# A two-layer decoder kernel: the gathered half of its expert layer taken first, and all gates of the dense half made from one-hots

## The chip, the cores and the metric

The program runs on one core of a Trainium2 chip. The metric is the device time of one execution in microseconds (us), lower is better. TensorE is called PE in the rows, VectorE DVE, ScalarE ACT, GpSimd POOL; SP is the queue that issues most DMAs.

## What is computed

A decoder of two layers over 512 tokens of width 1024, all in fp32. Each layer has three mixers (attention, delta rule, S5), whose results are gated, summed and projected ("combining"), then an expert layer, then a gated embedding. The change is about the combining and the expert layer, cut here to its core:

```python
x = x + (g_a * y_a + g_b * y_b + g_c * y_c) @ w_out          # combining
qry = (xt @ w_query)                                          # 8 heads, two parts of 128
v1, i1 = top_k(qry1 @ keys1, 16); v2, i2 = top_k(qry2 @ keys2, 16)
top_s, pos = top_k(v1[:, None] + v2[None, :], 16)             # 16 of 256 pairs
idx = i1 * 128 + i2                                           # one of 16384 experts
gate = softmax(top_s)
act = gelu(einsum('td,thkd->thk', xt, expert_u[idx]))
out = einsum('thk,thkd->td', gate * act, expert_v[idx])
x = x + out
```

A token thus uses 8 x 16 = 128 rows of `expert_u` and of `expert_v`, of 4 KB each.

## The kernel before

The 512 tokens are four tiles of 128, in two halves. Both halves need the same expert layer, but get it in two ways, at the same time.

- **The dense half** (half 0, tiles 0 and 1) is multiplied with all 16384 experts. These are 128 blocks of 128, two to a pair. `pre(p)` multiplies a pair's blocks of `expert_u` with the tokens (32 matmuls of 256 columns in the profile, L1645); ScalarE takes the gelu into one of 12 buffers (L1838); DVE multiplies by the gates, which are zero where a token has not chosen an expert (`values`, L2029 and L2032); `values(p)` on PE multiplies by the blocks of `expert_v` and sums in four banks (16 matmuls of 512 columns, L1657).
- **The gathered half** (half 1, tiles 2 and 3) fetches the rows that its tokens chose, with indirect DMAs from POOL (L2091): a job is one head of one tile, 16 fetches of 128 rows (512 KB) from each table. `chunk(c)` is four fetches: DVE takes four dot products with u rows (L1990) and, two chunks behind, adds four scaled v rows to x (L1996, L2002); ScalarE's gelu is between (L1805). There are 64 chunks, and rings of 5 buffers for u and for v, so fetching is at most five rows ahead.

`tail_order()` writes one list of steps by hand, and each engine walks the same list and does its part of each step. So the place of a step in the list is its place in each engine's queue, and its DMAs' place in SP's. The steps:

- `gate`, `mix`, `out`: combining. A half is four times three gates (L1549, each a 1 MB panel of weights) and a mix (three products into two banks that DVE reads, L1888, L1892), then four `out` panels (L1577, L1897).
- `norm`, `query`, `score`: normalize, multiply by a 1 MB panel (L1603), multiply by the keys (L1614).
- `choose(k, part)`: one head of one half on DVE, in four parts, from L1918 to L1981: some 50 instructions, one after another.
- `slots`, `hot(q)`: the gates of tile 1 as a matrix [expert, token]. PE transposes the chosen numbers; then for four tokens at a time (a quad) DVE makes two one-hots (L2016, L2018), ScalarE scales one by the gates (L1817), PE multiplies them (L1632), ScalarE copies the product (L1823) and stores 2 MB each 8 quads (L1826). The gates of tile 0 go another way: POOL scatters them one by one into an array in DRAM (L2101), which the mixer phase has filled with zeros (L721).
- `add`: DVE adds the dense sums to x (L2039), in the list behind chunk 56. Behind it come the last chunks and the embedding.

The order now: combining of the dense half; its norm; combining of the gathered half, with all eight heads of the dense half chosen beside it; norm of the gathered half, one head chosen; `slots` and 32 quads, with chunks 0 to 3 and five `pre` among them; seven `pre`; then `values` and `pre` of 64 pairs beside chunks 4 to 55; chunks 56 to 63. A `values(p)` step on DVE gates pair p + 2, if its gelu is there; PE's `values(p)` waits for the gates. The list holds the steps in the ratio of 64 pairs to 52 chunks.

Of the kernel before, what the change touches and what calls it, by code (L numbers as in the profile page):

```python
# [17 lines left out]
F32 = mybir.dt.float32  # L18
# [570 lines left out]
def phase_attend(m, layer):  # L589
# [5 lines left out]
    with ExitStack() as ctx:  # L595
        s = semaphores(m, COMMON + " soft_ready exp_done o_filled o_ready ur_ready scanned x_ready y_done y_read gelu_done zeros_set cells_cleared")
        sb = lambda n, shape, dt=F32: ctx.enter_context(nc.sbuf_tensor(f"{n}_{layer}", shape, dt))
        small = sb("small2", [P, 64])
        zeros = sb("zeros", [P, ZEROS])
# [125 lines left out]
        @block.gpsimd  # L725
        def _(pool):
            nc.gpsimd.memset(zeros[:, :], 0.0).then_inc(s.zeros_set, 1)

# [614 lines left out]
CELLS = P * KEYS * P  # L1343
CELL_OCT = OCT * P
LATE_CHUNKS = 4
# [3 lines left out]
def tail_order():  # L1349
# [7 lines left out]
    order = steps[0] + [("norm", 0), ("query", 0, 0)]  # L1357
    second = iter(steps[1])
    for head in range(PEER_HEADS):
        if head + 1 < PEER_HEADS:  # L1360
            order.append(("query", 0, head + 1))
        order.append(("score", 0, head))
        order += [("choose", head, part) for part in (0, 1)]
        order.append(next(second))
        order += [("choose", head, part) for part in (2, 3)]
        if head >= 2:
            order.append(next(second))
    order += list(second)
    order += [("norm", 1), ("query", 1, 0), ("query", 1, 1), ("score", 1, 0)]
    order += [("choose", PEER_HEADS, part) for part in range(4)]  # L1370
    order += [("score", 1, 1), ("slots",)]
    beside = {}
    for head in range(2, PEER_HEADS):
        at = HEAD_CHUNKS * (head - 1) - (4 if head == PEER_HEADS - 1 else 0)
        beside.setdefault(at - 5, []).append(("query", 1, head))
        beside.setdefault(at - 2, []).append(("score", 1, head))

    def chunk(c):
        out = beside.pop(c, []) + [("chunk", c)]
        head = c // HEAD_CHUNKS + 1  # L1380
        if c % HEAD_CHUNKS < 4 and head < PEER_HEADS - 1:
            out.append(("choose", PEER_HEADS + head, c % HEAD_CHUNKS))
        if c % HEAD_CHUNKS >= 4 and head == PEER_HEADS - 2:
            out.append(("choose", CHOICES - 1, c % HEAD_CHUNKS - 4))
        return out

    pairs = 0
# [846 lines left out]
```

## Time and profile before

| | |
|---|---|
| median of 3 runs | 4261.98 us (4260.22 to 4263.0) |
| the profiled run, its own time | 4251.53 us |
| span of its instructions | 4249.7 us |
| PE busy | 3756.1 us, 88% |
| DVE busy | 2619.1 us, 62% |
| ACT busy | 811.9 us, 19% |
| POOL busy | 1856.3 us, 44% |
| bytes moved by DMA | 1063.93 MB, 250 GB/s on average |

The profile is one execution. Busy time counts instructions that an engine is working on; a matmul's end is modelled, and neighbours overlap, so the time that a row of matmuls costs is read from start to start. Idle time is shown with what ended it. A share of busy time over the whole span mixes stages with different limits, so the stages are read one by one.

### The profile page before, as it was taken

The page shows a single profiled execution, that of the slowest core. Times are in us where ns is not written, and L with a number is a line of the kernel's source. Part 1 is how long each engine was busy: PE and PEld are TensorE (multiplying, and loading weights), DVE is VectorE, ACT ScalarE, POOL GpSimd, SP SyncE. Part 2 cuts the span into 40 slices and gives each one's busy share as a digit, 9 for nine tenths or more (in the row PEclk, how much of TensorE's full clock was granted, in tenths as well). Part 3 has the DMA queues.
Part 4 walks back from the last instruction along what each step waited for, and adds up shares of the span by engine and source line. Part 5 has one row for each costly group of instructions (what it writes and reads, how often), then busy time and mean ns, then how long its engine had stood idle before and what let it go on. Part 6 is the DMA issues. An engine that isn't in the chain of part 4 may idle for free. (4 is left out here: it accounts for less than half of the span.)

```text
span 4249.7 us, 42972 instructions
## 1 busy us (share of the span) xinstructions
PE 3756.1 (88%) x15498; PEld 2778.5 (65%) x15498; DVE 2619.1 (62%) x5356; ACT 811.9 (19%) x1637; POOL 1856.3 (44%) x1714
## 2 busy tenths in 40 slices
PE   8889998978999999993697899989789999999935
PEld 7546787867766666641585467877676666666424
DVE  5765216645577677788657652166456776677876
ACT  2243302224000000000222532022240000000002
POOL 6102004764455455567370020047645554555663
PEclk9889999989999999996798999999899999999967
DMA  3201144558999999999722012345579999999996
GB/s 103 109 30 40 66 139 119 125 142 268 376 406 409 409 407 409 407 397 378 266 82 109 31 39 76 139 119 124 159 253 397 405 410 409 401 409 409 399 381 253
DMA packets 333955, 1063.93 MB, mean 250 GB/s; under 512 B 79152, under 2 KB 96176, under 8 KB 312496
## 3 DMA queue, kind: packets, MB, share of 16 engines
q0 software_dynamic: 184320, 537.08, 34.5%
q1 hardware_dynamic: 132368, 505.22, 31.5%
q10 hardware_dynamic: 17056, 18.88, 1.3%
q8 instruction: 124, 2.03, 0.2%
q14 instruction: 87, 0.71, 0.0%
HBM read 1025.27 MB, written 35.78 MB: 250 GB/s over the span
## 5 line engine op out<-in xcount | busy, mean ns | idle before, releaser
L2091 POOL DMA_INDIRECT u_rows<-in_peer_u,idx_all x512 | 662.7, 1294 | 681.1 <-DVE act_u L1990 564.3
L1657 PE MATMUL bank<-v_tile,shared 128*128 128x512 f32 x2048 | 904.6, 597 | 25.3 <-DVE shared L2032 22.5
L2002 DVE SCALAR_TENSOR_TENSOR x<-v_rows,act_w,x 128x1024 f32<-128x1024 f32 x512 | 657.9, 1285 | 345.0 <-DMA v_rows<-in_peer_v,idx_all 325.9
L2091 POOL DMA_INDIRECT v_rows<-in_peer_v,idx_all x512 | 545.7, 1066 | 402.2 <-DVE x L2002 309.8
L1657 PEld LDWEIGHTS bank<-v_tile,shared 128*128 128x128 f32 x2048 | 392.0, 192 | 476.5 <-issue 444.3
L1990 DVE CUSTOM_DVE_ANT_0 u_rows<-u_rows,h 128x1024 f32<-128x1024 f32 x512 | 609.2, 1223 | 146.1 <-DMA u_rows<-in_peer_u,idx_all 144.7
L2101 POOL DMA_INDIRECT first_cells<-first_gate,cell_all x256 | 412.1, 1610 | 578.0 <-DVEq L1982 465.3
L1645 PE MATMUL bank<-hT,bT 128*128 128x256 f32 x2048 | 454.4, 381 | 0.0
L1645 PEld LDWEIGHTS bank<-hT,bT 128*128 128x128 f32 x2048 | 391.1, 191 | 73.6 <-issue 23.9
L1549 PE MATMUL bank<-hT,ring 128*128 128x256 f32 x1536 | 341.3, 384 | 14.2 <-PEq L150 14.2
L1549 PEld LDWEIGHTS bank<-hT,ring 128*128 128x128 f32 x1536 | 294.3, 193 | 55.9 <-issue 15.8
L1315 POOL TENSOR_TENSOR dn_ct<-dn_lt,mixer_consts 128x512 f32<-128x512 f32 x48 | 64.1, 1336 | 595.7 <-ACT dn_lt L1127 461.2
L1838 ACT ACTIVATE shared<-bank 128x512 f32<-128x512 f32 x128 | 76.1, 595 | 1023.3 <-PE bank L1657 949.8
L1645 PE MATMUL bank<-hT,aT 128*128 128x256 f32 x1024 | 234.7, 383 | 0.0
L1603 PE MATMUL bank<-hT,ring 128*128 128x256 f32 x1024 | 228.8, 383 | 3.5 <-issue 3.5
L1645 PE MATMUL bank<-hT,sT 128*128 128x256 f32 x1024 | 231.5, 379 | 0.0
L1645 PEld LDWEIGHTS bank<-hT,aT 128*128 128x128 f32 x1024 | 196.0, 193 | 38.9 <-issue 14.3
L1603 PEld LDWEIGHTS bank<-hT,ring 128*128 128x128 f32 x1024 | 197.0, 193 | 36.2 <-issue 9.8
L1645 PEld LDWEIGHTS bank<-hT,sT 128*128 128x128 f32 x1024 | 195.0, 190 | 26.0
L1888 DVE TENSOR_TENSOR shared<-shared,bank 128x512 f32<-128x512 f32 x48 | 32.5, 687 | 252.3 <-PE bank L1549 250.9
L1691 PE MATMUL bank<-ring,shared 128*128 128x256 f32 x512 | 129.5, 417 | 39.5 <-issue 37.6
L1670 PE MATMUL bank<-consts,shared 128*128 128x128 f32 x64 | 14.3, 407 | 168.1 <-issue 120.5
(377 smaller groups left out, 4998.9 us busy)
## 6 DMA issues: line engine op xcount, KB each, us to landing
v_tile<-in_peer_v SPq DMA_DIRECT2D x256, 512.0 KB, 7.5
ring<-in_w_in_panels SPq DMA_DIRECT2D x76, 1024.0 KB, 4.9
bT<-in_peer_ut SPq DMA_DIRECT2D x128, 512.0 KB, 7.5
ring<-in_peer_w_query SPq DMA_DIRECT2D x32, 1024.0 KB, 5.0
aT<-in_peer_ut SPq DMA_DIRECT2D x64, 512.0 KB, 6.9
sT<-in_peer_ut SPq DMA_DIRECT2D x64, 512.0 KB, 6.8
ring<-in_ple_w_gate SPq DMA_DIRECT2D x24, 1024.0 KB, 8.4
first_cells<-zeros SPq DMA_DIRECT2D x16, 1024.0 KB, 11.4
```

The source lines that it names most:

```text
L1315: nc.gpsimd.tensor_tensor(heads(ct[:, i % 2, :]), heads(lt[:, i % NT, :]), over(m.c(f"join{JOINS[i // NT]}").unsqueeze(1), (P, DN, P)), AL ...
L1549: ins = mm(bank[:, cols(mt)], a[:, mt * P:(mt + 1) * P], b[:, cols(half)], start=(n == 0), stop=(n == len(groups) - 1))
L1603: ins = mm(bank[:, cols(part)], w[:, k, part * P:(part + 1) * P], m.hT[:, k, cols(half)], start=(k == 0), stop=(k == KD - 1))
L1645: ins = mm(m.banks[2 + p % 2][:, cols(e % 2)], pre_w[e % DENSE][:, k, :], m.hT[:, k, cols(0)], start=(k == 0), stop=(k == KD - 1))
L1657: ins = mm(acc[t][part][:, :], act_pair[p % AHEAD][:, at:at + P], v_tile[:, e % DENSE, part * 512:part * 512 + 512], start=(e == 0), stop= ...
L1691: ins = mm(bank[:, cols(t)], ple_hT[:, k, t * P:(t + 1) * P], w[:, k, :], start=(k == 0), stop=(k == KD - 1))
L1838: f(act_pair[p % AHEAD], m.banks[2 + p % 2][:, :], ACT.Gelu_apprx_tanh).then_inc(s.pre_read, 1)
L1888: tt(sig[:, br, :], sig[:, br, :], bank[:, :], ALU.mult).then_inc(s.vec_read, 1)
L1990: nc.vector.tensor_tensor_reduce(out=u[:, n % RINGS, :], in0=u[:, n % RINGS, :], in1=h[:, t, :], scale=1.0, scalar=0.0, op0=ALU.mult, op1= ...
L2002: stt(out=m.x[:, 2 + t, :], in0=vr[:, n % RINGS, :], scalar=act_w[:, p % 4, i:i + 1], in1=m.x[:, 2 + t, :], op0=ALU.mult, op1=ALU.add).the ...
L2091: nc.gpsimd.indirect_dma_start(out=rows[:, n % RINGS, :], out_offset=None, in_=table, in_offset=bass.IndirectOffsetOnAxis(ap=idx_all[:, t, ...
L2101: nc.gpsimd.indirect_dma_start(out=cells, out_offset=bass.IndirectOffsetOnAxis(ap=cell_all[:, n:n + 1], axis=0), in_=first_gate[:, 0, n:n ...
```

## The change

- The gathered half is combined first, the dense half second. Beside the dense half's combining three heads of the gathered half are chosen, and chunks 0 to 10 run.
- Then come the dense half's norm, chunk 11, and all eight of its heads, each with a `query`, a `score` and (six times) a `pre` between them.
- `slots` and `hot` now cover both dense tiles: 64 quads. A scaled one-hot is made by one `tensor_scalar` for each token on DVE (compare, then multiply by the gate); of each three quads' second one-hots ScalarE makes one, by a square and a relu, and DVE two. Chunks 12 to 15 stand behind quads 15, 31, 47 and 63.
- The scatter, the array of cells, its zeros and the `token` numbers go. The gates come in one 1 MB load for each 8 blocks, the first two of them behind `pre(8)` in SP's list, and one DVE instruction gates a pair.
- Behind the last six `pre` comes chunk 16, and 64 pairs stand beside chunks 17 to 55. The gathered half's fourth head is chosen from chunk 17 on. `add` stays behind chunk 56.
- ScalarE's gelu of a chunk moves behind the next chunk's place in the list. POOL walks the list too.

```diff
             Panels(m, s, []).stream(sp, input_panels(io, layer, "deltanet"))
-            sp.wait_ge(s.zeros_set, 1)
-            n = KEYS // ZERO_PARTS
-            for k in range(ZERO_PARTS):
-                sp.dma_start(io.cells[layer, :, n * k:n * (k + 1), :].rearrange("p e t -> p (e t)").rearrange("p (r z) -> p r z", z=ZEROS),
-                             over(zeros[:, :].unsqueeze(1), (P, n * P // ZEROS, ZEROS))).then_inc(s.cells_cleared, 16)
-            sp.wait_ge(s.cells_cleared, 16 * ZERO_PARTS)
...
-            nc.gpsimd.memset(zeros[:, :], 0.0).then_inc(s.zeros_set, 1)
...
-BLOCKS = P // STORE_T
-ZEROS = 512
-ZERO_PARTS = 8
+BLOCKS = 2 * P // STORE_T
 OCT = 8
 OCT_PAIRS = OCT // 2
-QUADS = P // 4
-HOT_CHUNKS = 4
+QUADS = 2 * P // 4
+HOT_CHUNKS = 17
+ACT_QUAD = 2
+GATES_AFTER = 8
+GATHER, DENSE_HALF = 1, 0
+FIRST_HEADS = 3
+CHOSEN = [(GATHER, head) for head in range(FIRST_HEADS)] + [(DENSE_HALF, head) for head in range(PEER_HEADS)]
+CHOSEN += [(GATHER, head) for head in range(FIRST_HEADS, PEER_HEADS)]
...
-    order = steps[0] + [("norm", 0), ("query", 0, 0)]
-    second = iter(steps[1])
+    place = {what: k for k, what in enumerate(CHOSEN)}
+    choose = lambda half, head: [("choose", place[half, head], part) for part in range(4)]
+    beside = {}
+    for head in range(FIRST_HEADS + 1, PEER_HEADS):
+    def chunk(c):
+        return beside.pop(c, []) + [("chunk", c)]
+
+    g, d = steps[GATHER], steps[DENSE_HALF]
+    order = g + d[0:1] + [("norm", GATHER)] + d[1:2] + [("query", GATHER, 0), ("query", GATHER, 1)] + d[2:3] + [("score", GATHER, 0)]
+    order += choose(GATHER, 0) + d[3:5] + [("score", GATHER, 1)] + choose(GATHER, 1) + d[5:6] + chunk(0) + d[6:7] + chunk(1)
+    begun = 2
+    for n in range(7, 20):
+        order += d[n:n + 1]
+        if n == 10:
+            order.append(("query", GATHER, 2))
+        if n == 11:
+            order += [("score", GATHER, 2)] + choose(GATHER, 2)
+        if n % 4 != 2 and n != 11:
+            order += chunk(begun)
+            begun += 1
+    order += [("norm", DENSE_HALF), ("query", DENSE_HALF, 0), ("query", DENSE_HALF, 1), ("score", DENSE_HALF, 0)] + chunk(begun)
+    begun += 1
+    pairs = 0
     for head in range(PEER_HEADS):
-        if head + 1 < PEER_HEADS:
-            order.append(("query", 0, head + 1))
-        order.append(("score", 0, head))
...
-    beside = {}
-    for head in range(2, PEER_HEADS):
-        at = HEAD_CHUNKS * (head - 1) - (4 if head == PEER_HEADS - 1 else 0)
...
+        order += [("query", DENSE_HALF, head + 2)] if head + 2 < PEER_HEADS else []
+        order += [("score", DENSE_HALF, head + 1)] if head + 1 < PEER_HEADS else []
+        order += choose(DENSE_HALF, head)
+        if pairs < EARLY:
+            order.append(("pre", pairs))
+            pairs += 1
+    order.append(("slots",))
     for q in range(QUADS):
         order.append(("hot", q))
-        if q % (QUADS // HOT_CHUNKS) == QUADS // HOT_CHUNKS - 1:
-            order += chunk(q // (QUADS // HOT_CHUNKS))
-        if q % 5 == 4 and pairs < EARLY:
-            order.append(("pre", pairs))
-            pairs += 1
+        if q % 16 == 15 and begun < HOT_CHUNKS - 1:
+            order += chunk(begun)
+            begun += 1
     order.append(("hot", QUADS))
     for p in range(pairs, AHEAD):
         order.append(("pre", p))
+        if p == GATES_AFTER:
+            order.append(("first_gates",))
+    while begun < HOT_CHUNKS:
+        order += chunk(begun)
+        begun += 1
+    for n, what in enumerate([("query", GATHER, FIRST_HEADS), ("score", GATHER, FIRST_HEADS)] + choose(GATHER, FIRST_HEADS)):
+        beside.setdefault(begun + n, []).append(what)
...
+                pe.wait_ge(*right_made(q))
                 if q >= 2:
                     pe.wait_ge(s.hot_read, q - 1)
                 for i in range(4):
...
+            def gate_oct(k):
+                if k >= 2:
+                    sp.wait_ge(s.gated, OCT_PAIRS * (k - 1))
+                sp.dma_start(gates[:, k % 2, :], dram[:, k].rearrange("p b e t -> p (b e t)")).then_inc(gate_in[k % 2], 16)
+
+            def first_gates():
+                for k in range(2):
+                    sp.wait_ge(stored[k], 16 * BLOCKS // 2)
+                for k in range(2):
+                    gate_oct(k)
...
+                c -= 1
+                if 0 <= c < CHUNKS:
                     act.wait_ge(s.u_free, STEP * (c + 1))
                     f(act_g[:, c % 4, :], act_u[:, c % 4, :], ACT.Gelu_apprx_tanh).then_inc(s.gelu_done, 1)
...
+                k = q + 2
+                if k < QUADS and by_act(k):
+                    if k >= 4:
+                        act.wait_ge(s.hot_filled, k - 3)
+                    tile, at = k // (P // 4), 4 * k % P
                     for i in range(4):
-                        at = 4 * q + i
-                        f(left[q % 4][:, i, :], left[q % 4][:, i, :], ACT.Copy, scale=turned_sel[:, 2, at:at + 1]).then_inc(s.left_scaled, 1)
+                        f(right[k % 4][:, i, :], m.c("iota"), ACT.Square, scale=-1.0, bias=turned_sel[:, tile, 0, at + i:at + i + 1]).then_inc(s.right_squared, 1)
+                    act.wait_ge(s.right_squared, 4 * right_made(k)[1])
+                    f(right[k % 4], right[k % 4], ACT.Relu, scale=-1.0, bias=1.0).then_inc(s.right_acted, 1)
...
-                at = 4 * q
-                tt(left[q % 4], over(turned_sel[:, 1, at:at + 4].unsqueeze(2), (P, 4, P)),
-                   over(m.c("iota").unsqueeze(1), (P, 4, P)), ALU.is_equal).then_inc(s.left_ready, 1)
-                tt(right[q % 4], over(turned_sel[:, 0, at:at + 4].unsqueeze(2), (P, 4, P)),
-                   over(m.c("iota").unsqueeze(1), (P, 4, P)), ALU.is_equal).then_inc(s.right_ready, 1)
+                tile, at = q // (P // 4), 4 * q % P
+                for i in range(4):
+                    ts(left[q % 4][:, i, :], m.c("iota"), turned_sel[:, tile, 1, at + i:at + i + 1], first_gate[:, tile, at + i:at + i + 1],
+                       ALU.is_equal, ALU.mult).then_inc(s.left_ready, 1)
+                if not by_act(q):
+                    tt(right[q % 4], over(turned_sel[:, tile, 0, at:at + 4].unsqueeze(2), (P, 4, P)),
+                       over(m.c("iota").unsqueeze(1), (P, 4, P)), ALU.is_equal).then_inc(s.right_ready, 1)
...
-                    a = act_pair[p % AHEAD].rearrange("p (e t) -> p e t", e=2)
-                    g = gates[:, o % 2, 0:CELL_OCT].rearrange("p (e t) -> p e t", e=OCT)[:, at:at + 2]
-                    tt(a[:, :, 0:P], a[:, :, 0:P], g, ALU.mult).then_inc(s.gated, 1)
+                        v.wait_ge(gate_in[o % 2], 16 * (o // 2 + 1))
+                    a = act_pair[p % AHEAD].rearrange("p (e b t) -> p e b t", e=2, t=STORE_T)
+                    g = gates[:, o % 2, :].rearrange("p (b e t) -> p e b t", b=BLOCKS, e=OCT)[:, at:at + 2]
                     tt(a, a, g, ALU.mult).then_inc(s.gated, 1)
...
-            def scatter(n):
-                nc.gpsimd.indirect_dma_start(
-                    out=cells, out_offset=bass.IndirectOffsetOnAxis(ap=cell_all[:, n:n + 1], axis=0),
-                    in_=first_gate[:, 0, n:n + 1], in_offset=None, compute_op=ALU.add,
-                ).then_inc(m.scattered, 16)
...
+            def norm(half):
+                if half == GATHER:
+                    for n in range(RINGS):
+                        fetch(n, s.u_free, u, tables[0], m.u_landed)
+                    for n in range(RINGS):
+                        fetch(n, s.v_free, vr, tables[1], m.v_landed)
+
+            def chunk(c):
                 for n in range(STEP * c + RINGS, STEP * (c + 1) + RINGS):
                     fetch(n, s.u_free, u, tables[0], m.u_landed)
                 for n in range(max(STEP * (c - LAG), 0) + RINGS, STEP * (c - LAG + 1) + RINGS):
                     fetch(n, s.v_free, vr, tables[1], m.v_landed)
```

## Rows read from the trace of the kernel before

**Rows 1.** Table of stretches: us, length, busy time by engine, PEclk, DMA share, GB/s.

```profile
2762.00:3004.00 242.00, 219.70 (x1009) 191.94 (x1008) 144.54 (x562) 51.70 (x90) 153.58 (x96) 0.95 0.50 126
...
3030.00:3046.00 16.00, 0.21 (x2) 0.00 (x0) 15.19 (x64) 2.41 (x7) 4.87 (x4) 0.63 0.10 0
...
3046.00:3147.00 101.00, 81.66 (x445) 72.31 (x446) 77.84 (x158) 60.91 (x174) 58.88 (x44) 0.91 0.83 278
...
3203.00:3940.00 737.00, 737.00 (x2633) 497.46 (x2632) 528.92 (x991) 56.34 (x134) 386.05 (x335) 1.00 1.03 407
...
4050.00:4098.00 48.00, 0.30 (x1) 0.00 (x0) 36.88 (x47) 0.82 (x4) 30.82 (x27) 0.55 1.01 396
```

**Rows 2.** Timeline, TensorE, dense sums: start us, us, engine, line, operation.

```profile
1405.19 7.03 PE L1657 MATMUL bank<-v_tile,shared 128*128 128x512 f32 x16
...
1412.05 7.07 PE L1645 MATMUL bank<-hT,bT 128*128 128x256 f32 x32
...
1418.96 7.03 PE L1657 MATMUL bank<-v_tile,shared 128*128 128x512 f32 x16
```

**Rows 3.** Timeline, TensorE and DVE, from the last pre to add, second layer.

```profile
3945.01 34.50 PE L1657 MATMUL bank<-v_tile,shared 128*128 128x512 f32 x80
...
4043.17 7.13 PE L1657 MATMUL bank<-v_tile,shared 128*128 128x512 f32 x16 [1.41 <-DVE shared L2032]
...
3944.76 0.15 DVE L1996 TENSOR_TENSOR act_w<-act_g,gate_all 128x4 f32<-128x4 f32 x1
...
4097.46 2.48 DVE L2039 TENSOR_TENSOR x<-x,bank 128x512 f32<-128x512 f32 x4
```

**Rows 4.** Timeline, TensorE and DVE: end of the first combining, first two choices.

```profile
2732.55 29.58 PE L1577 MATMUL bank<-ring,shared 128*128 128x256 f32 x128 [2.90 <-DVE shared L1892]
...
2787.51 0.87 DVE L1918 MAX8 sel_v<-scores 128x8 f32<-128x128 f32 x4 [15.82 <-ACT scores L1793]
...
2803.52 0.87 DVE L1918 MAX8 sel_v<-scores 128x8 f32<-128x128 f32 x4
```

**Rows 5.** Timeline, DVE: first and last instructions of a mix beside choosing.

```profile
2835.66 1.28 DVE L1888 TENSOR_TENSOR shared<-shared,bank 128x512 f32<-128x512 f32 x2 [0.22 <-DVE first_gate L1981]
...
2842.13 0.69 DVE L1892 TENSOR_TENSOR shared<-shared 128x512 f32<-128x512 f32 x1
```

**Rows 6.** Timeline, DVE: the first instruction of chunk 56.

```profile
4087.23 1.22 DVE L1990 CUSTOM_DVE_ANT_0 u_rows<-u_rows,h 128x1024 f32<-128x1024 f32 x1
```

**Rows 7.** Timeline, DVE, then TensorE: norm, choice, first one-hot, last query, first values.

```profile
3009.47 1.29 DVE L1905 SCALAR_TENSOR_TENSOR h<-x,small,gain_ffn 128x1024 f32<-128x1024 f32 x1
...
3029.59 0.87 DVE L1918 MAX8 sel_v<-scores 128x8 f32<-128x128 f32 x4 [15.77 <-ACT scores L1793]
...
3045.31 0.69 DVE L2016 TENSOR_TENSOR gain_ffn<-turned_sel,consts 128x512 f32<-128x512 f32 x1
...
3147.42 7.07 PE L1603 MATMUL bank<-hT,ring 128*128 128x256 f32 x32
...
3202.68 7.03 PE L1657 MATMUL bank<-v_tile,shared 128*128 128x512 f32 x16
```

**Rows 8.** Timeline, ScalarE, then TensorE: quads of one-hots.

```profile
3053.39 1.27 ACT L1817 ACTIVATE gain_ffn<-gain_ffn,turned_sel 128x128 f32<-128x128 f32 x4
...
3055.03 1.27 ACT L1817 ACTIVATE gain_ffn<-gain_ffn,turned_sel 128x128 f32<-128x128 f32 x4
...
3068.68 2.08 PE L1632 MATMUL bank<-shared,gain_ffn 128*128 128x128 f32 x8 [2.01 <-ACT gain_ffn L1817]
...
3071.05 2.08 PE L1632 MATMUL bank<-shared,gain_ffn 128*128 128x128 f32 x8 [0.30 <-ACT gain_ffn L1817]
```

**Rows 9.** DMA issues: source, queue, count, KB each, median us to landing.

```profile
dense_gates<-v_tile ACTq DMA_DIRECT2D x4, 2048.0 KB, 11.2
```

**Rows 10.** A DVE cast in the timeline, and a group of POOL (busy, mean ns).

```profile
3035.53 0.20 DVE L1935 CAST sel_if<-sel_i 128x64 f32<-128x64 uint32 x1
...
L2091 POOL DMA_INDIRECT u_rows<-in_peer_u,idx_all x512 | 662.7, 1294 | 681.1 <-DVE act_u L1990 564.3 <-issue 96.9 <-DVEq L1982 19.9
```

More of the change, by code:

```diff
@@ L1368, in tail_order @@
[L1368 to L1371, printed above, removed]
-    beside = {}
-    for head in range(2, PEER_HEADS):
-        at = HEAD_CHUNKS * (head - 1) - (4 if head == PEER_HEADS - 1 else 0)
[L1375 to L1385, printed above, removed]
@@ L1387, in tail_order @@
-    pairs = 0
+    place = {what: k for k, what in enumerate(CHOSEN)}
+    choose = lambda half, head: [("choose", place[half, head], part) for part in range(4)]
+    beside = {}
+    for head in range(FIRST_HEADS + 1, PEER_HEADS):
+        at = HEAD_CHUNKS * (head - 1) - (4 if head == PEER_HEADS - 1 else 0)
+        beside.setdefault(at - 5, []).append(("query", GATHER, head))
+        beside.setdefault(at - 2, []).append(("score", GATHER, head))
+        for part in range(4):
+            beside.setdefault(at + part, []).append(("choose", place[GATHER, head], part))
@@ L1482, in phase_tail @@
         ple_hT = comb
+        normed = [ple_h, h]
+        rank = lambda half: 1 - half
+        done = lambda half, head: (s.selected if half == GATHER else s.first_chosen, head + 1)
         act_pair = [shared[:, k, :] for k in range(AHEAD)]
@@ L1526, in slot, with by_act, right_made @@
             return t, head * TOPK + n % TOPK
+        def by_act(q):
+            return q % 3 == ACT_QUAD
+        def right_made(q):
+            mine = len([k for k in range(q + 1) if by_act(k) == by_act(q)])
+            return (s.right_acted if by_act(q) else s.right_ready), mine
         def arrivals(n):
@@ L1558, in mix @@
             def mix(half, pair):
-                if half == 0 and pair == 0:
+                if rank(half) == 0 and pair == 0:
                     pe.wait_ge(s.wg_in, 16)
@@ L1571, in out @@
                 if n == 0:
[L1572 removed]
+                    pe.wait_ge(s.comb_ready, KD // 2 * (rank(half) + 1))
                 w = panel()
@@ L1582, in norm @@
             def norm(half):
-                for t in range(2 * half, 2 * half + 2):
-                    pe.wait_ge(s.h_ready, t + 1)
+                for t in range(2):
+                    pe.wait_ge(s.h_ready, 2 * rank(half) + t + 1)
                     for part, banks in ((0, to_act), (1, to_vec)):
@@ L1593, in query @@
             def query(half, head):
-                if half == 0 and head == 0:
+                if rank(half) == 0 and head == 0:
                     pe.wait_ge(s.keys_in, 16 * 2)
@@ L1613, in score @@
                         at = 2 * t + part
-                        ins = mm(bank[:, at * KEYS:(at + 1) * KEYS], qry[:, head % 2, part * HALF_T + t * P:part * HALF_T + (t + 1) * P], keys[:, part, :],
+                        ins = mm(bank[:, at * KEYS:(at + 1) * KEYS], qry[:, CHOSEN.index((half, head)) % 2, part * HALF_T + t * P:part * HALF_T + (t + 1) * P], keys[:, part, :],
                                  start=True, stop=True)
@@ L1751, in _ @@
             loads = iter(range(len(sources)))
-            parts = {"gate": panel, "mix": panel, "out": panel, "query": panel, "embedded": panel, "pre": pre, "values": values, "add": add}
+            parts = {"gate": panel, "mix": panel, "out": panel, "query": panel, "embedded": panel, "pre": pre,
+                     "first_gates": first_gates, "values": values, "add": add}
             for what, *n in order:
@@ L1764, in gate @@
             def gate(half, pair, br):
-                if br == 0 and half + pair:
-                    act.wait_ge(s.comb_ready, KD // 2 * half + pair)
+                if br == 0 and rank(half) + pair:
+                    act.wait_ge(s.comb_ready, KD // 2 * rank(half) + pair)
                 bank = banks.take()
@@ L2117, in _ @@
                     fetch(n, s.v_free, vr, tables[1], m.v_landed)
-                if c < LATE_CHUNKS:
-                    for n in range(TOPK // LATE_CHUNKS):
-                        scatter(late + c * TOPK // LATE_CHUNKS + n)
+            parts = {"norm": norm, "chunk": chunk}
+            for what, *n in order:
+                if what in parts:
+                    parts[what](*n)
     clear(nc, s)
```

131 lines of the change are left out of this document (38 added, 93 removed).

## The prediction

> **What bounds the kernel now.** All times are those of the second layer in the profiled run, unless another is said; both layers run alike. The first view is the table of stretches [rows 1]. From 3203 to 3940 (the dense sums) TensorE is busy 737 of 737 us and DMA moves 407 GB/s: both are full. Which of them binds is read in TensorE's timeline [rows 2]: a pair's values take 6.86 us (1405.19 to 1412.05) and a pair's `pre` 6.91 us, and they follow each other without a gap. The sum agrees: 51 values, 51 `pre`, five queries of 6.91 and five scores of about 0.9 are 742 us, and the last `pre` ends at 3945.0 [rows 3], 742.3 us behind the first values at 3202.7 [rows 7]. So up to the last `pre` TensorE sets the pace and DMA only just keeps up. Behind it this turns: 13 values (89 us) are left, but DVE is in the middle of chunk 46 (its `act_w`, the eleventh from the end of chunk 56 backwards) and must end chunk 56 before `add`. TensorE ends at 4050.3 and `add` starts at 4097.5, 152.5 us behind the last `pre` [rows 3]: 14.4 us for each of 10.5 chunks, DMA at 396 GB/s to the end [rows 1]. These 63 us beyond TensorE's work are all that chunks cost in this stage. In front of the dense sums the chain is: combining (TensorE), norm and first queries, choosing (DVE), one-hots, seven `pre`.
>
> **The change, part by part.** I place each step on the second layer's clock.
>
> *Combining.* The gathered half is combined first; its cost is unchanged, to 2762.1 [rows 4]. Then one gate panel (32 matmuls as a `pre`, 6.9 us) goes in front of the norm, one behind it and one behind the two queries; of these 21 us about 5 cover the norm's wait. The first choice thus starts not at 2787.5 but near 2803.5. From there DVE is the longer engine: three choices at 16.0 us (2787.51 to 2803.52 [rows 4]) are 48.1; four mixes, each 7.2 us when TensorE's third product must wait for DVE to read a bank (2835.66 to 2842.8 [rows 5]), 28.8; four sums of `out`, 2.8; chunks 0 and 1 have only a u part, 4.6 each, 9.2; chunks 2 to 10 at 10.2 us (4087.23 to 4097.46 [rows 3, 6]), 91.8; the norm 2.8; one wait of 7 for the second head's score. That is 190.5, to 2994. TensorE's own work is 219.7 us in the old stretch less five queries and scores (5 x 7.9), 180 us, so to 2942: DVE binds. DMA has 11 chunks (47 MB with what is ahead in the rings) and some 18 panels (19 MB) in 183 us, 88% of what 409 GB/s would carry; I add 8 us for waits: 3002. Transposes, two queries and the score then take as long as before (DVE's norm to the choice, 3010.8 to 3029.6, 18.8 us [rows 7]), with chunk 11 under them: the dense half's first choice starts at 3021, where one starts now at 3029.6. Minus 9, with ends of minus 34 (25 less, somewhat under half the gap to TensorE's pace) and minus 3 (6 us more of DMA waits).
>
> *Choosing.* Now one choice stands between 3029.6 and the one-hots at 3045.3 [rows 7]; the seven other dense heads are hidden beside the second combining. After the change all eight stand there and nothing else fills DVE: 8 x 16.02 = 128.2, plus 112.5 us. TensorE does six queries and six `pre` under them, about 15.0 us a head, so DVE stays the longer. The extra sums of `chosen` and `listed` swap one for one. Slots: now hidden behind the last choice; then six transposes and two copies, 2.5 us by the 0.6 us copies, plus 2.5.
>
> *One-hots.* Now 32 quads, four chunks and five `pre` take 102.1 us, 3045.3 to 3147.4 [rows 7]. Alone a quad costs 1.64 us, 3053.39 to 3055.03, ScalarE's four scalings and one copy [rows 8]. After: 64 quads. ScalarE has a copy (0.5) each and in one of three four squares (1.27, the row of the scalings) and one relu over 512 (0.6, the copy's row) with a wait: 1.25 a quad. DVE has four 128x128 `tensor_scalar` each and in two of three a 128x512 comparison (0.6 between starts). The trace has no such `tensor_scalar`; below it stands the 128x64 cast at 0.20 [rows 10], of which about 0.1 is apart from the next; above it half the comparison's step, 0.3. I take 0.2, near the casts, for 1.2 a quad. Storing bounds it too: eight stores of 2 MB, 11.2 us to landing [rows 9], over two buffers, so a block of eight quads needs 11.7 us. Three chunks of 10.2 stand between quads (the fourth behind the last); four buffers hide 3 us of each. Five blocks at 11.7, three at 17: 110, and 2 us of lower clock after each chunk: 116. Bounds: 100 if nothing but 1.25 a quad and 20 us of chunks count, 167 below. Plus 14.
>
> *To the first values.* Seven `pre`, 48.4 us, as now; the query that stands there (3147.42 [rows 7]) is gone, minus 6.9. The gates load earlier in SP's order, but SP waits there for the last store (11.2 us) and has 2 MB to bring, all under four `pre`; where SP stands, only weights of `pre` 9 are queued behind, needed 20 us later. Cost nothing; 10 us if that cover is short. The removed scatter of tile 0's gates (POOL's 128 issues a layer) and the clearing of its array in DRAM lie beside other work: nothing. First values: 3202.7 - 9 + 112.5 + 2.5 + 14 - 6.9 = 3315.7, plus 113.
>
> *The dense sums.* 39 chunks instead of 52, but the same values, `pre` and five queries: 742 us to the last `pre`. DMA would need 306 MB, 750 us for the whole, so it has slack there and the slack is worth nothing. One gating instruction instead of two frees only DVE. The gain is behind the last `pre`: there DVE stands at chunk 48 or 49. It can't be further ahead, since ScalarE's gelu of a chunk now sits behind the next chunk, and ScalarE follows TensorE's `pre`. Eight chunks at 14.4 are 115, less 12 to 15 us for rings that are full: `add` starts 100 us after the last `pre` instead of 152.5. Minus 52; bounds minus 62 (TensorE's 90 us) and minus 34 (no ring ahead).
>
> *After `add`* nothing changes (152 us).
>
> *Sum.* Per layer 113 - 52 = +61, twice +122: 4251.5 + 122 = 4373.5 for a run like the profiled one, whose own time lies 10.5 us under the median of three; so 4384.
>
> **The rivals.**
> *TensorE paces the new combining* (faster). For it: it is the busy engine there now (219.7 of 242). It would take the dense half's first choice to 2963, 58 us before my 3021, and one-hots at their lower bound, 16 us less: 61 - 74 = -13 a layer, 4384 - 148 = 4236. It turns the sign only from 61 us on; DVE's 190 us of listed work against 180 speak against it. 14%.
>
> *One-hots at TensorE's lower level, 1.2 of 2.4 GHz* (slower still). The granted clock is 0.63 in the stretch of the choice and 0.91 beside the one-hots, where five `pre` of 6.9 us lie between quads [rows 1]. After short idle times there a quad's eight matmuls take 2.08 us and the quads come 2.37 us apart [rows 8], against 1.64 else. The change takes every `pre` out of this stage. 64 x 2.37 = 152 and 15 for chunks are 167: +51 a layer, 4486. 12%. The Trainium skill (TensorE: Matmul & The Clock Gate, What's actually happening) says the lower level is the default and activity releases it; the rows agree.
>
> *No saving behind the last `pre`.* If DVE's lead is lost or rings are empty: +18 (the bound) to +52 a layer, 4420 to 4488. 7%.
>
> *`tensor_scalar` and POOL's issues hold each other up.* Some 34 gather issues of about 1.2 us [rows 10] fall among 256 of the new instructions; if each issue stops DVE, up to 41 us of DVE time a layer, of which I count 30 on the path: 4444. 7%. The Trainium skill (SBUF — State Buffer, SBUF: two separate sides) says that Vector instructions in a two-port mode and GpSimd lock each other out of a shared port; the trace of before has no such pair to check it.
>
> *It comes out even*: TensorE's pace in the combining alone, the one-hots as forecast, 4384 - 116 = 4268. 6%.
>
> **Numbers.** Forecast 54%, 4384. A measurement here can tell 0.2% from no change. Faster 14%, same 6%, slower 80%. My own case with its bounds: combining -25, one-hots -16, tail -10 a layer gives 4282; +6, +20 and +18 gives 4472. The range leaves out the first rival and the even case: 4295 to 4490.
>
> **What would show it.** Eight choices of 16 us in a row on DVE with TensorE at 90% and DMA almost still; first values 100 to 130 us later in each layer; the same 742 us from there to the last `pre`, with DMA under 400 GB/s; `add` within 15 us of TensorE's last values. I am wrong if the dense half's first choice starts much before 3000, if the one-hots take under 100 us or over 150, or if the stage with `pre` gets shorter than 742, for then DMA was binding it.

## The result and the profile after

The changed kernel takes 4495.75 us (median of 4, 4488.75 to 4500.43) against 4261.1 for the one before: ratio 1.055, 95% interval 1.0532 to 1.0568. The forecast was 4384 (4295 to 4490): the direction held, the size was half of what came, and the time lies above the range. The profiled run took 4500.43 us (span 4498.5) where the one of before took 4251.53 (span 4249.7): 248.8 us more in the span, 126.2 by the end of the second layer's first combining and 122.6 behind it. As the layers run alike, all that follows is the second layer, read from that point on (2762.1 before, 2888.1 after).

The table of stretches of the changed kernel shows the stages in order (us; length; busy time of TensorE, its weight loads, DVE, ScalarE, POOL; granted clock; DMA share; GB/s), to be held against [rows 1]:

```profile
2888.00:3117.00 229.00, 184.07 (x809) 158.96 (x808) 148.98 (x336) 47.75 (x72) 92.55 (x76) 0.90 0.71 265
3117.00:3163.00 46.00, 21.40 (x93) 18.39 (x92) 31.24 (x41) 6.96 (x13) 25.21 (x23) 0.70 0.98 369
3163.00:3288.00 125.00, 90.40 (x445) 79.97 (x444) 117.04 (x488) 32.07 (x64) 0.00 (x0) 0.87 0.28 103
3288.00:3413.00 125.00, 73.37 (x513) 68.69 (x513) 122.80 (x341) 74.39 (x175) 31.57 (x25) 0.83 0.62 219
3413.00:3482.00 69.00, 51.11 (x227) 44.32 (x226) 36.33 (x51) 4.87 (x9) 34.59 (x27) 0.85 0.91 347
...
3482.00:4223.00 741.00, 741.00 (x2647) 499.61 (x2646) 410.81 (x766) 55.11 (x122) 316.11 (x247) 1.00 0.89 343
4223.00:4346.00 123.00, 90.11 (x211) 39.63 (x209) 80.69 (x107) 2.11 (x10) 73.37 (x61) 0.88 1.03 409
```

While eight heads are chosen and while the one-hots are made, DVE is busy 240 of 250 us and DMA moves 103 and 219 GB/s. In the sums TensorE is full and DMA has 16% to spare (343 GB/s, of the 409 that it moves in the stage behind), where it was full before (407). Bytes were moved out of the stage that could carry them into stages where DVE pays for them.

By the prediction's steps, in us of the second layer:

| step | before | predicted | after |
|---|---|---|---|
| end of first combining to the dense half's first choice | 267.5 | 258.5 | 275.0 |
| choices and slots, to the first one-hot | 15.7 | 130.7 | 125.7 |
| one-hots | 102.1 | 116 | 124.1 |
| to the first values | 55.3 | 48.4 | 68.9 |
| dense sums to the last `pre` | 742.5 | 742 | 741.6 |
| last `pre` to `add` | 152.3 | 100 | 122.8 |
| `add` to the end | 152.2 | 152 | 152.1 |

Four rows are off by 16.5, 8, 20.5 and 23 us to the worse, and one by 5 to the better. The four are taken in turn.

*Front.* DVE's timeline at the end of the combining (start us, us, engine, line, operation, in brackets the idle time before it and what ended it):

```profile
3117.91 1.28 DVE L2008 SCALAR_TENSOR_TENSOR x<-v_rows,act_w,x 128x1024 f32<-128x1024 f32 x1
3120.37 1.28 DVE L2008 SCALAR_TENSOR_TENSOR x<-v_rows,act_w,x 128x1024 f32<-128x1024 f32 x1 [1.18 <-DMA v_rows<-in_peer_v,idx_all]
...
3140.01 1.28 DVE L1919 SCALAR_TENSOR_TENSOR shared<-x,small,gain_ffn 128x1024 f32<-128x1024 f32 x1
...
3163.32 0.87 DVE L1932 MAX8 sel_v<-scores 128x8 f32<-128x128 f32 x4 [7.42 <-ACT scores L1807]
```

and what DVE waited for from its first choice to the norm, 207 us (us in all, times, longest):

```profile
DVE sel_v L1932 <- ACT scores L1807: 36.1, 2, 28.6
DVE shared L1902 <- PE bank L1558: 13.1, 4, 3.3
DVE x L2008 <- DMA v_rows<-in_peer_v,idx_all: 8.6, 7, 2.4
DVE u_rows L1996 <- DMA u_rows<-in_peer_u,idx_all: 7.9, 8, 1.6
```

Gathered rows held DVE up for 16.5 us, not the 8 that were added for it. (The 28.6 in the first line is the wait in front of the first choice.) TensorE was done with its last `out` product at 3117.6 and idled 23.8 us.

*One-hots.* DVE's timeline among the quads (x4: four instructions in a row):

```profile
3294.91 1.11 DVE L2023 TENSOR_SCALAR gain_ffn<-consts,turned_sel,first_gate 128x128 f32<-128x128 f32 x4
3295.94 0.69 DVE L2026 TENSOR_TENSOR shared<-turned_sel,consts 128x512 f32<-128x512 f32 x1
3296.54 1.11 DVE L2023 TENSOR_SCALAR gain_ffn<-consts,turned_sel,first_gate 128x128 f32<-128x128 f32 x4
3297.57 1.11 DVE L2023 TENSOR_SCALAR shared<-consts,turned_sel,first_gate 128x128 f32<-128x128 f32 x4
3298.59 0.68 DVE L2026 TENSOR_TENSOR shared<-turned_sel,consts 128x512 f32<-128x512 f32 x1
```

Four `tensor_scalar` are 1.03 us from start to start (3294.91 to 3295.94), 0.257 each where 0.2 was taken, and with two comparisons of 0.6 in three quads a quad is 1.43 on DVE. 64 x 1.43 are 91.3; three chunks of 10.2 come on top in full, since DVE itself is the longest engine: 122. The stores, by which the prediction paced the stage (11.2 us to landing), took 7.7 in the median (the profile's page has it for one of the two buffers), and no engine waited for one in this stage.

*To the first values.* The chain of waits, in order of time:

```profile
3413.91 23.13 DMA dense_gates<-gates
...
3437.05 0.02 SPq L1745
...
3437.12 0.33 SPq L1741
...
3437.49 0.43 SPq L1741
...
3437.96 13.76 DMA bT<-in_peer_ut
...
3451.86 30.31 PE bank L1657 x128
```

The last store needed 23.1 us beside the gathers of two chunks. SP stood in `first_gates` until then, and the weights of `pre` 9 were issued behind 2 MB of gates and took another 13.8. TensorE idled 17.9 us and its next `pre` took 9.59 us instead of 7.07, at a granted clock of 0.50 (the lower level) while it had idled.

*Behind the last `pre`.* It ends at 4223.6 with DVE in chunk 49 (a `u` row, its four `v` rows and chunks 50 to 56 are left, 7.7 chunks), as forecast. But these took 122.8 us, 16.0 each, not 14.4.

### The profile page after: what moved, and what is told of

Its sections match the earlier page's. It is cut to its first block and busy times, and to the rows that moved or that the text cites. A ratio compares the mean times of both kernels' runs of the same rounds, so it can differ in the third digit from the quotient of the medians.

```text
span 4498.5 us, 44058 instructions
## 1 busy us (share of the span) xinstructions
PE 3840.9 (85%) x16016; PEld 2854.8 (63%) x16016; DVE 2700.5 (60%) x5614; ACT 877.4 (20%) x1677; POOL 1523.2 (34%) x1456
## 5 line engine op out<-in xcount | busy, mean ns | idle before, releaser
L2096 POOL DMA_INDIRECT u_rows<-in_peer_u,idx_all x512 | 679.8, 1328 | 1610.4 <-DVE act_u L1996 988.5
L2096 POOL DMA_INDIRECT v_rows<-in_peer_v,idx_all x512 | 608.0, 1188 | 626.3 <-DVE x L2008 488.6
L1996 DVE CUSTOM_DVE_ANT_0 u_rows<-u_rows,h 128x1024 f32<-128x1024 f32 x512 | 603.3, 1223 | 91.3 <-DMA u_rows<-in_peer_u,idx_all 81.9
L2002 DVE TENSOR_TENSOR act_w<-act_g,gate_all 128x4 f32<-128x4 f32 x128 | 20.3, 159 | 471.7 <-ACT act_g L1820 471.7
L361 PE MATMUL bank<-ring,hT 128*128 128x256 f32 x640 | 151.4, 398 | 0.0
```

What stands on the lines that cost most here:

```text
L361: ins = nc.tensor.matmul(bank[:, 0:PANEL], m.hT[:, k, r::4], w[:, k, :], start=(k == 0), stop=(k == KD - 1))
L1996: nc.vector.tensor_tensor_reduce(out=u[:, n % RINGS, :], in0=u[:, n % RINGS, :], in1=h[:, t, :], scale=1.0, scalar=0.0, op0=ALU.mult, op1= ...
L2096: nc.gpsimd.indirect_dma_start(out=rows[:, n % RINGS, :], out_offset=None, in_=table, in_offset=bass.IndirectOffsetOnAxis(ap=idx_all[:, t, ...
```

## Experiments

A ratio is the time over that of the kernel before, measured beside it. Differences from the changed kernel are taken from two ratios; each has an interval of some 8 us to either side, so a difference of 16 us is one only roughly. What a stage takes is read from the second layer of each trace.

### Gates later in SP's list

```
-GATES_AFTER = 8
+GATES_AFTER = 11
```

> The changed kernel, but the first two loads of gates stand behind pre(11) in SP's list and not behind pre(8). Theory, the place in the list: SP stands there for the last store (issued at 3413.9, landed at 3437.0), and pre 9's weights are queued behind it and behind 2 MB of gates, so that TensorE idles 17.9 us and runs the next pre slower. With the loads three pre later the store has landed before SP comes to them: first pre of the run to first values 50 to 52 us instead of 68.9, 18 us less a layer, 4460. Rival, the bytes: 2 MB of gates, the chunks' gathers and the weights must all come in before the first values, and DMA is the limit wherever they stand: the stall moves to the first values, 4490 to 4500.

Measured: 4470.56 us, ratio 1.0509 (1.0491 to 1.0527), against 1.055 for the changed kernel: 17 us less, and 28 less between the profiled spans. First `pre` to first values 54.9 us instead of 68.9. SP's and TensorE's rows:

```profile
3429.24 0.80 SPq L1741 DMA_DIRECT2D gates<-dense_gates  x2
```

```profile
3444.06 6.32 PE L1657 MATMUL bank<-hT,aT 128*128 128x256 f32 x16 [3.64 <-DMA aT<-in_peer_ut]
```

The gates are issued without standing behind the store, and the stall of 17.9 is 3.6. So the place in the list was the larger part of the 20.5 us. The rest is probably bytes (389 GB/s in this stretch); no run separates it. The expected 18 us a layer was 14.

### Fewer chunks behind the last pre

```
-        goal = min(PAIRS_ALL, -(-(c - HOT_CHUNKS + 1) * PAIRS_ALL // (DENSE_END - HOT_CHUNKS)))
+        goal = min(PAIRS_ALL, PAIRS_ALL if c >= DENSE_END else -(-(c - HOT_CHUNKS + 1) * SPREAD // (DENSE_END - HOT_CHUNKS)))
```

with `SPREAD = 54`.

> The changed kernel, but chunks 17 to 55 are spread over 54 pairs instead of 64, so that 4 chunks instead of 9 stand behind the last pre in the list. Theory: the stage before the last pre has DMA to spare (343 of 409 GB/s), and behind it a chunk costs only its own bytes, 4.2 MB or 10.3 us, over a fixed 44 us of values and panels. 742 us to the last pre as before at some 385 GB/s, then TensorE's 13 values bind: add 93 us behind the last pre instead of 122.9, 30 us less a layer, 4436. Rival: DMA has no real slack there, since gathers and loads hold each other up: the stage to the last pre grows by what the end loses, 4485 to 4500.

Measured: 4428.69 us, ratio 1.0412 (1.0394 to 1.0429), 59 us less than the changed kernel by the ratios. The stretches up to the last `pre` and from there to `add`:

```profile
3445.00:4186.00 741.00, 741.00 (x2648) 499.60 (x2647) 468.07 (x839) 55.67 (x128) 371.59 (x293) 1.00 0.97 378
4186.00:4276.00 90.00, 89.74 (x211) 39.59 (x209) 25.48 (x37) 0.88 (x4) 22.01 (x18) 1.00 0.80 302
```

The sums take the chunks at no cost, with 378 GB/s, and `add` follows TensorE's last values at once. So DMA's slack in front of the last `pre` is real. What is behind it goes by bytes: one fixed part and 10.3 us (4.2 MB at 409 GB/s) for each chunk. Before, 152.3 us went to 10.5 chunks, after, 122.8 to 7.7: 10.5 us a chunk, with 42 to 44 us left at none (13 MB of values alone are 33 us at 409 GB/s). Two points always give a line, but the other orders lie on it too. 44 us and 10.3 a chunk make 131.6 for the 8.5 chunks left in the next two experiments, which took 133.2 and 132.3; and 117.1 and 120.2 for the 7.1 and 7.4 left in the runs of the kernel before with its chunks earlier and with five chunks among its quads, which took 116.4 and 119.9. Only the run with three chunks beside the `pre`s lies off, 116.4 for 7.6 chunks where the line has 122.3. With the few chunks left in this run TensorE's 90 us bind.

### Quads without chunks

```
-HOT_CHUNKS = 17
+HOT_CHUNKS = 13
```

> The changed kernel, but chunks 12 to 14 don't stand between the 64 quads of one-hots and chunk 16 not behind the last pre's: they go with the dense sums (43 chunks there instead of 39). Theory: DVE is the longest engine of the one-hots (1.43 us a quad), so each chunk there costs its full 10.3 us: stage of 94 us instead of 124. The sums have DMA to spare, so the moved chunks cost nothing before the last pre and one more of them, 10 us, behind it: 20 us less a layer, 4456. Rival, bytes are conserved: what leaves the one-hots comes back behind the last pre, 4490 to 4500. Rival, TensorE: without work between them the quads fall to 2.37 us each, stage 150, 4550.

Measured: 4444.36 us, ratio 1.0446 (1.0428 to 1.0463), 44 us less than the changed kernel. The one-hots:

```profile
3263.00:3357.00 94.00, 68.35 (x507) 64.03 (x508) 93.95 (x304) 71.15 (x168) 0.92 (x1) 0.94 0.47 157
```

DVE is busy in all of the 94 us: it is the pace, and each of the three chunks had cost its 10 us. TensorE kept a clock of 0.94, so the rival of the lower level is out. The last `pre` to `add` grew by 10.4 us, the price of the one chunk more. The run beats the 4456 expected: without the chunk behind the last `pre`s, first `pre` to first values took 61.4 us instead of 68.9.

### Four chunks less beside the combining

```
-        if n % 4 != 2 and n != 11:
+        if n in (7, 8, 9, 12, 13):
```

with `HOT_CHUNKS = 13`.

> The changed kernel, but with 7 chunks beside the dense half's combining instead of 11; the one-hots keep their three, so 43 chunks stand with the dense sums. Theory: DVE paces the combining (TensorE's last out product ends at 3117.5, DVE comes to the norm at 3140.0, with 16 us of waits for gathered rows between). With four chunks less DVE is done before TensorE: the norm comes some 19 us earlier and then TensorE binds; one more chunk behind the last pre costs 10: 9 us less a layer, 4478. Rival, the waits for the score and the banks pace it: front unchanged, 10 us more a layer, 4516.

Measured: 4469.3 us, ratio 1.0513 (1.0496 to 1.0531), 16 us less than the changed kernel. TensorE's last `out` product ends 229.2 us behind the first combining in both; but the norm follows it at once:

```profile
3102.81 0.69 DVE L1911 TENSOR_TENSOR x<-x,bank 128x512 f32<-128x512 f32 x1 [6.22 <-PE bank L1586]
3106.32 0.16 DVE L1918 RECIPROCAL small<-small 128x1 f32<-128x1 f32 x1 [2.82 <-ACT small L1792]
```

The dense half's first choice comes at 254.3 instead of 275.0. So at 11 chunks DVE binds, at 7 TensorE does. But its pace isn't that of the prediction's rival, which had the choice at 201 (2963 on the clock of before): TensorE, whose work is some 180 us, needs 229 to its last `out` product, above all since in each mix it waits for DVE to read a bank. The last mix, in the changed kernel and in this one:

```profile
3081.52 3.58 PE L1558 MATMUL bank<-sT,ring 128*128 128x256 f32 x8 [10.22 <-DVE shared L1902]
```

```profile
3066.50 3.78 PE L1558 MATMUL bank<-sT,ring 128*128 128x256 f32 x8 [10.69 <-DVE shared L1902]
```

Four such waits are 36 us (10.2, 8.4, 7.2 and 10.2 in the changed kernel), with or without chunks between. The combining in the new order (229, with three queries in it) is shorter than in the old (242, with eight); it is the chunks laid on it that make the front longer.

### The new gates in the old order

The changed kernel with `tail_order` of the kernel before, 64 quads with a `pre` behind every tenth, chunks behind quads 15, 31, 47 and 63, and

```
-        normed = [ple_h, h]
-        rank = lambda half: 1 - half
+        normed = [h, h]
+        rank = lambda half: half
```

> The changed kernel's gates (64 quads with tensor_scalar, no scatter, one gating instruction, late gelu) in the order of the kernel before: the dense half first, seven of its heads chosen beside the second combining, four chunks beside the quads, five or six pre's among them. It splits the change. Theory: DVE paces the quads, 64 x 1.43 and 30 for three chunks and 16 for a head's choice, 138 us, then six pre's with the stall at the gates, 60: 198 us from the first one-hot to the first values instead of 157, 41 us a layer, and nothing else moves: 4254 + 82 = 4336. So 82 of the change's 234 us would be the gates and the rest the order. Rival, the old scatter and the second gating instruction cost something on the path: 4300 or less.

Measured: 4346.61 us, ratio 1.0204 (1.0187 to 1.0221); expected 4336. From the first one-hot to the first values 203.7 us against 157.3, of which 154.1 are up to the first `pre` behind the quads. The rest is smaller: last `pre` to `add` 156.3 against 152.3, the second combining 236.6 against 242.2. The stretches from the first one-hot to that `pre`, and from the last `pre` to `add`:

```profile
3090.00:3244.00 154.00, 118.40 (x736) 108.57 (x737) 135.07 (x401) 77.65 (x177) 42.55 (x34) 0.92 0.74 251
...
4036.00:4193.00 157.00, 94.53 (x210) 40.45 (x208) 123.89 (x182) 6.01 (x18) 102.31 (x84) 0.83 1.02 402
```

So the gates (with the late gelu) cost 88 of the change's 234 us, and the new order the other 146.

### The kernel before: chunks earlier in the sums

> The kernel before, with its 52 chunks spread over 58 pairs instead of 64, so that 8 chunks instead of 12 stand behind the last pre: the edit that gained 30 us a layer in the changed kernel. Theory, here DMA is full on both sides of the last pre (407 and 396 GB/s): what the end gains the stage before it loses, last pre some 20 to 30 us later, add in its place: 4254. Rival, only DVE's lead sets the 152 us at the end: add 111 us behind the last pre and that one in its place, 4172.

The edit is that of the changed kernel's `goal` in the second experiment, with `SPREAD = 58` beside the old constants. Measured: 4265.48 us, ratio 1.0014 (1.0005 to 1.0024). Up to the last `pre`, and from there to `add`:

```profile
3212.00:3996.00 784.00, 752.27 (x2656) 506.80 (x2655) 575.30 (x1069) 62.03 (x144) 431.14 (x365) 0.98 1.02 402
3996.00:4113.00 117.00, 95.17 (x210) 40.66 (x208) 78.42 (x114) 2.04 (x8) 74.80 (x59) 0.93 1.03 409
```

784.7 instead of 742.5, then 116.4 instead of 152.3, 6 us more together: what gains 30 us a layer in the changed kernel gains nothing here and costs a little, since DMA has nothing to spare. The Trainium skill (Perfetto Trace Analysis, Roofline) puts the ceiling of one core's DMA engines at about 435 GB/s. The traces here stay below it: stretches of 100 us, laid every 20 us over all the runs, reach 411 at most, with DMA's share at 1.03. For these transfers, rows gathered beside loads, 409 is the figure to plan with.

### The kernel before: chunks into its own gaps

```
+    begun = HOT_CHUNKS
     for p in range(pairs, AHEAD):
         order.append(("pre", p))
+        if p in BESIDE_PRE:
+            order += chunk(begun)
+            begun += 1
```

with `BESIDE_PRE = (6, 8)` and the sums' `goal` spread over 61 pairs.

> The kernel before, with chunks 4 and 5 beside the last pre's in front of the dense sums (behind pre(6) and pre(8)), and the sums' list spread so that 10 chunks stand behind the last pre instead of 12. In that stretch (3147 to 3203) DVE waits 44 us and DMA moves 270 of 409 GB/s. Theory, the sums with their end are a matter of bytes there (364 MB at 407 GB/s): two chunks less are 8.4 MB, 20 us a layer: 742 us to the last pre as before, add 132 behind it instead of 152, 4214. Rival, the chunks' gathers delay the gates and weights of the first values by as much: 4254, no change.

Measured: 4226.56 us, ratio 0.993 (0.9913 to 0.9946). The stretch in front of the first values and the two behind:

```profile
3129.00:3196.00 67.00, 64.39 (x308) 56.60 (x307) 37.63 (x60) 9.35 (x23) 37.51 (x29) 1.00 0.97 365
3196.00:3939.00 743.00, 742.71 (x2657) 501.18 (x2658) 542.99 (x1029) 59.50 (x140) 397.15 (x337) 1.00 1.03 408
3939.00:4071.00 132.00, 98.72 (x208) 41.61 (x206) 93.03 (x131) 2.33 (x10) 81.74 (x70) 0.90 1.01 400
```

19.8 us less behind the last `pre`, as expected; 6 of them are given back between the first one-hot and the first values (163.6 against 157.3), so 4214 was missed by 13 us.

> The kernel before, with three chunks beside the last pre's (behind pre(6), pre(8) and pre(10)) instead of the two of the earlier run, 9 chunks behind the last pre. With two, DMA moved 366 GB/s in that stretch: 60 us x 43 GB/s are 2.6 MB, less than a chunk's 4.2. Theory, bytes: the third brings 0 to 6 us a layer over the two (4226 there against 4258 for the kernel before): 4214 to 4226. Rival, the third holds up the weights of the last pre's: first values 10 us later, 4240 or more.

With `BESIDE_PRE = (6, 8, 10)` and `SPREAD = 60`: 4213.78 us, ratio 0.9901 (0.9885 to 0.9918), at the better end of what was expected. Against two chunks there the sums get 6 us longer and their end 16 shorter.

> The kernel before, with five chunks between its 32 quads instead of four (behind quads 6, 12, 18, 24 and 31) and two beside the last pre's. Beside those quads DVE is busy 78 of 101 us and ScalarE paces them (1.64 us a quad), and DMA moves 278 GB/s, so a chunk isn't paid in full there, unlike in the changed kernel: theory 5 us for the fifth chunk against 10 us of bytes less behind, 4216. Rival, a chunk there costs its 10.3 us as in the changed kernel: 4226, as with two beside the pre's alone.

```
-HOT_CHUNKS = 4
+HOT_CHUNKS = 5
+HOT_AT = (6, 12, 18, 24, 31)
...
-        if q % (QUADS // HOT_CHUNKS) == QUADS // HOT_CHUNKS - 1:
-            order += chunk(q // (QUADS // HOT_CHUNKS))
+        if q in HOT_AT:
+            order += chunk(HOT_AT.index(q))
```

With `BESIDE_PRE = (7, 9)` and `SPREAD = 60`: 4200.89 us, ratio 0.9872 (0.9856 to 0.9888), the fastest of all. One-hots, `pre`s, sums, and their end:

```profile
3019.00:3119.00 100.00, 80.21 (x431) 70.84 (x432) 85.34 (x175) 58.40 (x166) 70.06 (x51) 0.90 0.89 305
3119.00:3183.00 64.00, 58.63 (x285) 51.69 (x284) 32.34 (x48) 9.09 (x23) 29.48 (x25) 0.99 0.98 382
3183.00:3927.00 744.00, 744.00 (x2648) 500.73 (x2648) 545.29 (x1034) 58.93 (x139) 403.45 (x339) 1.00 1.02 406
3927.00:4047.00 120.00, 95.82 (x210) 40.89 (x208) 80.78 (x113) 2.13 (x9) 71.79 (x61) 0.91 1.03 410
```

The fifth chunk lengthens the one-hots by 3 to 6 us and not by 10.3: up to the `pre` in front of the last quad they take 99.8 us, against 93.4 in the kernel before and 96.6 in the run with two chunks beside the `pre`s, both with four chunks. DVE has 15 of 100 us to spare even now, where it has 2 of 125 in the changed kernel. From the first one-hot to the first values it is 163.2 us, as in that run (163.6), so all told the chunk came free, and 4216 was beaten by 15 us. The end of the sums is 32 us shorter than before.

### All four edits on the changed kernel

```
-HOT_CHUNKS = 17
+HOT_CHUNKS = 9
-GATES_AFTER = 8
+GATES_AFTER = 11
+SPREAD = 58
...
-        if n % 4 != 2 and n != 11:
+        if n in (7, 8, 9, 12, 13):
```

and the `goal` of the second experiment.

> All four edits on the changed kernel at once, five chunks deeper: gates behind pre(11), seven chunks beside the combining, none among the quads, one beside the last pre's, 47 with the dense sums, spread so that the last seven stand behind the last pre. Theory, the savings add up until DMA is full: front 254 (from the end of the gathered half's combining to the choice), 126 choosing, 95 quads, 52 to the first values, 742 and 91 for 339 MB at 407 GB/s, 152 at the end: 1512 us a layer where the kernel before has 1488: 4303. Rival, at that fill gathers and loads hold each other up: the sums with their end take 860, 4360.

Measured: 4325.6 us, ratio 1.0164 (1.0147 to 1.0181).

```profile
3324.00:4066.00 742.00, 742.00 (x2652) 500.29 (x2651) 513.82 (x900) 56.10 (x133) 391.18 (x330) 1.00 1.01 401
4066.00:4169.00 103.00, 91.26 (x208) 39.46 (x206) 64.18 (x86) 1.60 (x7) 58.13 (x49) 0.95 1.03 409
```

The savings add up (some 165 of the 234 us come back) until DMA is full; sums and end take 845 us where 833 were forecast. What stays is the bare choosing, 110 us a layer; the front (254.9 against 267.5), the one-hots with the `pre`s behind them (143.4 against 157.3) and the sums with their end (845 against 895) give back 76 of it.

## Why the prediction was right in sign and wrong in size

The sum per layer was forecast at 61 us and came to 122.6. The bounds by stage were right (DVE in the combining and the choosing, TensorE in the sums) except in the one-hots. The terms that failed are, by size, the end of the sums (23 us short), the loads of gates in front of the first values (20.5), the waits in the combining (16.5) and the one-hots (8).

*What bounds the kernel before.* Right, and its consequence was drawn too weakly. "DMA only just keeps up" was shown to be a limit: chunks earlier in the sums gain nothing. The 63 us "beyond TensorE's work" are bytes.

*Combining: minus 9, measured plus 7.5.* That DVE binds was right. The rival in which TensorE paces was priced far too high (58 us less than the forecast): with four chunks less it does pace, and comes to 254.3, 4 us less than the forecast, as it waits 36 us for banks. In the forecast itself the term that failed is the waits: the first choice came 3.5 us later than worked out, gathered rows held DVE 16.5 us instead of 8, and the two queries behind the norm took 15.9 us instead of 14, TensorE having idled 23.8 us (granted clock 0.70 in that stretch). That is 14 of the 16.5 us; the rest is spread over small waits.

*Choosing: plus 115, measured plus 110.* Right; eight heads without a mix between them are 15.4 us each, not 16.0. Slots plus 2.6, as forecast.

*One-hots: plus 14, measured plus 22.* The `tensor_scalar` was taken as 0.2 from a 128x64 cast and is 0.257. The larger fault is which resource binds: the stage was paced by stores at 11.2 us each, though two buffers give a store the time of the next block to land, and half of each chunk was hidden under them. The stores held nobody up, DVE binds, and chunks there are paid in full. That the total is off by 8 us only is luck: DVE needs 11.4 us for a block of eight quads (8 x 1.43), nearly the 11.7 that the stores had been given, so the chunks, 15 us too cheap, are what is left, less the 6 us put down to a lower clock. The rival of the lower clock did not come: TensorE had 0.83 here and its quads are not the longest.

*The port rival* is out. Four `tensor_scalar` beside POOL's issues of gathers, in DVE's timeline and in POOL's:

```profile
3322.19 1.11 DVE L2023 TENSOR_SCALAR gain_ffn<-consts,turned_sel,first_gate 128x128 f32<-128x128 f32 x4
3323.22 0.69 DVE L2026 TENSOR_TENSOR shared<-turned_sel,consts 128x512 f32<-128x512 f32 x1
```

```profile
3322.00 1.09 POOL L2096 DMA_INDIRECT v_rows<-in_peer_v,idx_all  x1 [0.30 <-issue]
3323.39 1.32 POOL L2096 DMA_INDIRECT v_rows<-in_peer_v,idx_all  x1 [0.31 <-issue]
```

The four take 1.03 us to the next instruction beside POOL as without it. Over the stage all of DVE's rows of four last 1.11 or 1.12 us, but one (1.20), and there are 25 of POOL's issues in it. Whether they run in the mode of which the Trainium skill (SBUF — State Buffer, SBUF: two separate sides) says that it locks POOL out, no run here shows.

*First values: minus 6.9, measured plus 13.6.* The prediction named the queue and what stands in it ("only weights of `pre` 9 are queued behind, needed 20 us later") and the price if the cover is short, 10 us. The step that failed is this cost of nothing. The cover was short because a store's landing was taken as 11.2 us from a median, and the last one, beside two chunks' gathers, took 23.1, and because the weights' own 13.8 us behind 2 MB of gates were not counted. Moving the loads showed it for 14 of the 20.5 us. That the gathers made the last store slow is likely but not tested by itself.

*Behind the last `pre`: minus 52, measured minus 29.5.* DVE's place (chunk 49) was right. Two steps failed. "14.4 us for each chunk" divides by the chunks a time of which 44 us don't depend on them: 44 + 7.7 x 10.3 are 123, where eight chunks at 14.4 are 115. That is 8 of the 23 us. The larger part, 15 us, is what full rings were to save: it didn't show, for the same line without such a credit fits both kernels. By bytes this is what one would expect, as DMA is full up to `add` in both, though no run tested the rings alone. The prediction had a bound for the case without them, minus 34; the measured minus 29.5 lies past it by what the fixed part adds.

*Dense sums and `add` to the end:* as forecast, to a microsecond. The slack in DMA was seen and called "worth nothing"; it was worth 60 us to whoever spread the list anew.

Left open: why the new gates in the old order shorten the second combining by 5.6 us a layer (3.2 of it are TensorE's shorter waits in three mixes, 4.1, 3.0 and 3.0 us instead of 6.0, 3.7 and 3.7), and how much of the 146 us for the order is the bare choosing and how much the chunks, beyond the sums above.

## What to carry to other kernels

Before work is moved, ask of each stage which resource is full: a chunk here cost 10 us beside one-hots paced by DVE, 3 to 6 beside those paced by ScalarE, and nothing in sums where DMA had slack. A time that is shared by counted items and a fixed load must not be divided by the items: fit a line through two points, or count bytes. And a load that waits for a store belongs behind everything that the next engine needs sooner.

## What the runs showed of the hardware

A 2 MB store landed 7.7 us after its issue in the median, and the last of the layer, beside two chunks' gathers, in 23.1. A row of 128x128 `tensor_scalar` with two scalars from SBUF took 0.257 us for each. Where it was full, one core's DMA moved 397 to 410 GB/s through 742 us of sums and through their end, and in no 100 us of any run more than 411.
